# A blocked triangular inverse whose levels are put together by predicated copies instead of identity products

## The chip, the cores and the metric

The kernel runs on one core of one Trainium2 chip. The metric is the device time of one execution in microseconds (us). Engines are named as in the profile: PE is the matrix engine (PEld its weight loads), DVE the vector engine, ACT the scalar engine, POOL the GpSimd engine, SP the one that queues weight loads from memory.

## What is computed

Two transformer blocks over 512 tokens of width 1024, in fp32. The first block mixes dilated window attention with an RWKV-7 recurrence of 16 heads of 64 channels; the change lies in that recurrence and nowhere else. Cut to what matters:

```python
def step(state, inp):                                   # one token, all heads
    r_t, w_t, k_t, v_t, kk_t, a_t = inp
    sa = jnp.einsum('bhij,bhj->bhi', state, -kk_t)
    state = (state * w_t[:, :, None, :]
             + sa[..., None] * (kk_t * a_t)[:, :, None, :]
             + v_t[..., None] * k_t[:, :, None, :])
    y_t = jnp.einsum('bhij,bhj->bhi', state, r_t)
    return state, y_t
...
mu = jnp.mean(y, axis=-1, keepdims=True)
var = jnp.mean(jnp.square(y - mu), axis=-1, keepdims=True)
y = ((y - mu) * lax.rsqrt(var + LN_X_EPS)).reshape(b, s, RWKV_WIDTH)
y = y * ln_w + ln_b
y = (y + bonus) * g
```

## The kernel before

**Chunks and the inverse.** The recurrence is worked in 4 chunks of 128 tokens, for 8 pairs of heads. Inside a chunk it needs the inverse of a unit triangular 128x128 matrix per head. Both heads of a pair share one square `Z` (one head in the upper triangle, the other in the lower, -1 on the diagonal), 4 chunks side by side: a tile of 128x512. The inverse is built in levels of blocks of 2, 4, 8, ... 128 rows. A level `lv` is one turn round three engines: PE multiplies the level's blocks of the gram by the inverse so far (`level_x`: 4 products of 128x128 into bank 5, L983), ACT copies the result to SBUF (`level`, L1483), PE multiplies by the inverse again, once for the inverse and once for its transpose (`level_t`: 2 groups of 4 products into banks 4 and 6, L995), and DVE multiplies each result by a mask of sides, `smask`, which gives the operands of the next level (`level_t` on DVE, L2148, tiles `tinv` and `tinv_t`).

The old inverse has to be added to each result. Before, PE does that: ACT copies each whole result to `Tb[1]` or `TT[1]` (`whole`, L1493), and each group of `level_t` begins with a product of that copy with the identity, 512 columns wide (L992). The level's blocks of the gram are cut out by DVE, one masked copy of `Z` into `Mb` per level (`level_mask`, L2131).

**Steps.** The code runs in steps p = -2 to 7. In one step, three pairs are under way at once: a = p goes through the chunks of the recurrence (`chunk_rhs`, `chunk_solve`, `chunk_out`), b = p + 1 gets its inverse, c = p + 2 gets its keys, decays and bonus. Steps 0 to 5 have all three. Every engine takes its instructions in the order in which they are written, so the order of the calls in each engine's `step(p)` sets everything.

**Fill.** Between these pieces PE works off projections of other columns ("side halves": 8 groups of 3 products, L583 to L585, of 0.7 us a group), at places counted (`fill()`, with `SLOTS3` in steps 0 to 4, `SLOTS2` in 5). A side half is gathered in one PSUM bank, bank 0, so the next one cannot begin before ACT and DVE have read the last (`take_half` on ACT, `shift_half` on DVE, L1969 and L1970). In steps 0 to 4 the second half of a step begins in the fill after `chunk_out` of chunk 2, the third in the fill before `level_x` of level 6; both wait for DVE's `shift_half`, at its place in DVE's own order.

**Low parts.** Each weight is split into a high and a low part; in this stretch ACT makes the high part (L1258) and DVE the low part (`weights_behind`, L2031), a 128x2048 subtraction. In steps 0, 2 and 4 there is one of these per step, just before DVE's first product mask of level 3 (`level_t(b, 3, 0)`). In steps 1, 3 and 5 there are two, one before level 2 and one before `level_t(b, 5, 0)`.

**Output.** When a pair's chunks are through, the raw output is copied from PSUM (`raw_out`, L1519), its mean over each head's 64 channels is taken by a PE product (`mean`, L952), DVE subtracts it (`centred`, L2186), ACT squares, PE sums (`variance`), and so on to `normed`.

## Time and profile before

| what | value |
|---|---|
| median of 3 runs | 1886.01 us (1885.96 to 1886.76) |
| profiled execution, its own time | 1888.21 us |
| its span, first to last instruction | 1886.4 us |
| PE busy | 1809.9 us, 96% |
| DVE busy | 829.4 us, 44% |
| ACT busy | 768.5 us, 41% |
| stretch of the inverses (steps -1 to 6) | about 297 to 723 us |
| length of steps 0 to 5 (start of one inverse to the start of the next) | 52.0 to 55.4 us |

The profile gives for each engine how long it was busy, and for each instruction when it began, how long it took, and what ended the idle time before it. Products are pipelined: one of 512 columns is shown with 0.39 to 0.45 us, but the next begins 0.23 us later, so starts have to be read, not lengths. The same holds for DVE and ACT, where an instruction of 0.69 us that nothing waits for is followed by the next after 0.60 us.

### The profile page before, as it was taken

The page shows a single profiled execution, that of the slowest core. Times are in us where ns is not written, and L with a number is a line of the kernel's source. Part 1 is how long each engine was busy: PE and PEld are TensorE (multiplying, and loading weights), DVE is VectorE, ACT ScalarE, POOL GpSimd, SP SyncE. Part 2 cuts the span into 40 slices and gives each one's busy share as a digit, 9 for nine tenths or more (in the row PEclk, how much of TensorE's full clock was granted, in tenths as well). Part 3 has the DMA queues.
Part 4 walks back from the last instruction along what each step waited for, and adds up shares of the span by engine and source line. Part 5 has one row for each costly group of instructions (what it writes and reads, how often), then busy time and mean ns, then how long its engine had stood idle before and what let it go on. Part 6 is the DMA issues. An engine that isn't in the chain of part 4 may idle for free.

```text
span 1886.4 us, 22629 instructions
## 1 busy us (share of the span) xinstructions
PE 1809.9 (96%) x9636; PEld 1482.6 (79%) x9636; DVE 829.4 (44%) x1206; ACT 768.5 (41%) x1126; POOL 514.0 (27%) x115
## 2 busy tenths in 40 slices
PE   6998998999999998998999999999999999999997
PEld 5896766888888787887888888787777788888886
DVE  2015526777877765434113344515864321113243
ACT  5235555556656643234223222434663342222222
POOL 2331200000000000342434444333334334444442
PEclk8999998999999999999999999999999999999999
DMA  4631222010001002432222222221213232222221
GB/s 159 217 116 46 79 87 64 26 48 26 26 28 44 23 34 80 155 134 101 89 99 103 89 98 103 90 99 68 71 64 112 78 112 90 97 104 90 98 103 67
DMA packets 54663, 161.19 MB, mean 85 GB/s; under 512 B 3327, under 2 KB 30335, under 8 KB 39844
## 3 DMA queue, kind: packets, MB, share of 16 engines
q1 hardware_dynamic: 42476, 135.40, 20.7%
q10 hardware_dynamic: 12088, 24.35, 3.8%
q8 instruction: 76, 1.25, 0.3%
q14 instruction: 23, 0.19, 0.0%
HBM read 153.16 MB, written 10.25 MB: 87 GB/s over the span
## 4 chain that ended last, share of the span: by engine, by line
PE 82%; DVE 8%; ACT 4%; issue 4%; DMA 1%; POOL 0%; ACTq 0%; DVEq 0%
PE ps L583 22%; PE ps L585 21%; PE ps L584 21%; PE ps L995 2%; PE ps L992 1%; DVE ht_lo L1888 1%; PE ps L1072 1%; PE ps L983 1%; PE ps L905 1%; PE ps L1036 1%; PE ps L910 1%; PE ps L703 1%; DVE x_res L1905 1%; ACT y_tok L1275 1%; PE ps L713 1%
## 5 line engine op out<-in xcount | busy, mean ns | idle before, releaser
L574 POOL TENSOR_TENSOR w_lo<-w_raw,w_hi 128x2048 fp32r<-128x2048 f32 x111 | 513.8, 4629 | 1341.9 <-ACT w_hi L1258 1341.9
L583 PE MATMUL ps<-ht_hi,w_hi 128*128 128x512 f32 (+1 forms) x1304 | 526.3, 404 | 21.8 <-DVE ht_lo L1888 10.9
L585 PE MATMUL ps<-ht_hi,w_lo 128*128 128x512 f32 (+1 forms) x1304 | 501.9, 385 | 0.0
L584 PE MATMUL ps<-ht_lo,w_hi 128*128 128x512 f32 (+1 forms) x1304 | 501.3, 384 | 0.0
L1258 ACT ACTIVATE w_hi<-w_raw 128x2048 fp32r<-128x2048 f32 x126 | 241.2, 1916 | 468.0 <-PE ps L585 414.3
L583 PEld LDWEIGHTS ps<-ht_hi,w_hi 128*128 128x128 f32 x1304 | 250.4, 192 | 82.0 <-issue 26.7
L585 PEld LDWEIGHTS ps<-ht_hi,w_lo 128*128 128x128 f32 x1304 | 250.0, 192 | 48.8
L584 PEld LDWEIGHTS ps<-ht_lo,w_hi 128*128 128x128 f32 x1304 | 250.8, 192 | 39.6 <-issue 1.7
L2342 DVE TENSOR_TENSOR hid_lo<-hidden,hid_hi 128x1024 fp32r<-128x1024 f32 x27 | 129.3, 4789 | 149.1 <-ACT hid_hi L1714 149.1
L583 PE MATMUL ps<-w_hi,hid_hi 128*128 128x512 f32 x432 | 168.2, 389 | 0.0
L585 PE MATMUL ps<-w_hi,hid_lo 128*128 128x512 f32 x432 | 168.1, 389 | 0.0
L584 PE MATMUL ps<-w_lo,hid_hi 128*128 128x512 f32 x432 | 168.1, 389 | 0.0
L583 PEld LDWEIGHTS ps<-w_hi,hid_hi 128*128 128x128 f32 x432 | 81.1, 188 | 16.9
L585 PEld LDWEIGHTS ps<-w_hi,hid_lo 128*128 128x128 f32 x432 | 81.1, 188 | 16.8
L584 PEld LDWEIGHTS ps<-w_lo,hid_hi 128*128 128x128 f32 x432 | 81.1, 188 | 16.7
L583 PE MATMUL ps<-w_hi,ht_hi 128*128 128x512 f32 (+2 forms) x256 | 86.2, 337 | 2.1 <-POOL w_lo L574 2.1
L585 PE MATMUL ps<-w_hi,ht_lo 128*128 128x512 f32 (+2 forms) x256 | 85.8, 335 | 0.0
L584 PE MATMUL ps<-w_lo,ht_hi 128*128 128x512 f32 (+2 forms) x256 | 85.8, 335 | 0.0
L2351 DVE TENSOR_TENSOR hidden<-ps,gate_act 128x1024 f32<-128x1024 f32 x16 | 19.6, 1224 | 133.1 <-ACT gate_act L1753 133.1
L1753 ACT ACTIVATE gate_act<-ps 128x1024 f32<-128x1024 f32 x16 | 16.5, 1029 | 123.4 <-PE ps L585 123.4
L2148 DVE TENSOR_TENSOR tinv<-ps,sides 128x512 fp32r<-128x512 f32 x48 | 33.1, 690 | 54.1 <-PE ps L995 51.3
L2438 DVE TENSOR_TENSOR hidden<-ps,hidden 128x1024 f32<-128x1024 f32 x11 | 13.5, 1224 | 95.7 <-PE ps L585 95.7
(308 smaller groups left out, 2569.6 us busy)
## 6 DMA issues: line engine op xcount, KB each, us to landing
w_raw<-in_wpack SPq DMA_DIRECT2D x114, 1024.0 KB, 4.8
w_raw<-in_wpack SPq DMA_DIRECT2D x24, 512.0 KB, 5.3
bias_skewed_dram<-bias_rows_dram ACTq DMA_DIRECT2D x1, 3840.0 KB, 23.0
toe<-bias_skewed_dram ACTq DMA_DIRECT2D x1, 3072.0 KB, 12.9
x_res<-in_x SPq DMA_DIRECT2D x4, 512.0 KB, 5.1
merged<-gate_dram ACTq DMA_DIRECT2D x2, 1024.0 KB, 9.1
gate<-gate_dram ACTq DMA_DIRECT2D x1, 2048.0 KB, 8.8
x_res<-in_x ACTq DMA_DIRECT2D x1, 2048.0 KB, 8.7
```

What stands on the lines that cost most here:

```text
L574: nc.gpsimd.tensor_tensor(Wl[:, slot, :], raw[:, slot, :], f32(Wh[:, slot, :]), ALU.subtract).then_inc(lo_ready, 1)
L583: mm(dst, wh, ah, start=first, stop=False)
L584: mm(dst, wh, al, start=False, stop=False)
L585: return mm(dst, wl, ah, start=False, stop=last)
L703: last = nc.tensor.transpose(ps[:, 7, j * P:(j + 1) * P], LG1[i % 2][:, e, (v0 + j) * P:(v0 + j + 1) * P], ident)
L713: last = mm(ps[HD * e:HD * e + HD, 7, 3 * P:4 * P], it["vals"][e][j], PT1[e][:, j, :], start=j == 0, stop=j == nv - 1)
L905: inc(mm(bank(1), LW[c % 2][rows, 0, :], FWA[rows, 0, :], start=True, stop=True), "z_full")
L995: last = mm(ps[:, (4, 6)[k], tok(t)], (tt, x)[k], (x, tt)[k], start=False, stop=t == NT - 1)
L1258: actf(Wh[:, n % RING, :], raw[:, n % RING, :], ACT.Copy).then_inc(hi_ready, 1)
L2148: inc(v.tensor_tensor((Tb, TT)[k][0][:], src, smask(lv - 1), ALU.mult), "t_ready")
L2342: v.tensor_tensor(HIl[:, 2 * g:2 * g + 2, :], HID[:, 2 * g:2 * g + 2, :], f32(HIh[:, g % RING, :, :]), ALU.subtract).then_inc(hid_lo, 1)
L2351: v.tensor_tensor(HID[:, 2 * u:2 * u + 2, :], ps[:, 2 * (d % 2):2 * (d % 2) + 2, :], SG[:], ALU.mult).then_inc(pair_taken[d % 2], 1)
```

## The change

The result of a level is no longer added on PE. Two tiles `Wf` (fp32, in the place of `Tb[1]` and `TT[1]`) hold the inverse and its transpose; ACT fills them once per pair after level 0. After each later level DVE copies the level's blocks out of PSUM into `Wf` under a mask (`copy_predicated`), waits for that to be complete, and multiplies `Wf` by the mask of sides. So the products may leave anything outside the level's blocks, and PE can multiply by the whole gram: `Mb` is one rounded copy of `Z` (`square`, on ACT), and the masks of levels 1 to 6 go. The last level's blocks are two half-tiles per result, copied by ACT (`last_blocks`), for which `head_inverses` waits. The values are centred per head as tokens, ahead of the recurrence (`centred_values`: a sum and a subtraction on DVE), so the raw output has mean zero, and `mean` and `centred` go. Three DVE instructions of `normed` become two.

```diff
+        Wf = [place(f"inverse{k}", [P, NT, P], at=r.at - 4 * NT * P * (3 - 2 * k))[0] for k in range(2)]
...
+                if lv == 1:
+                    w("whole_ready", 4, b, 2)
                 for k in range(2):
-                    w("whole_ready", 2 * (nl - 1), b, 2 * lv - 1 + k)
-                    mm(bank((4, 6)[k]), identR[:], (Tb, TT)[k][1][:].rearrange("p t c -> p (t c)"), start=True, stop=False)
                     for t in range(NT):
                         x, tt = Xb[:, t, :], TT[0][:, t, :]
-                        last = mm(ps[:, (4, 6)[k], tok(t)], (tt, x)[k], (x, tt)[k], start=False, stop=t == NT - 1)
+                        last = mm(ps[:, (4, 6)[k], tok(t)], (tt, x)[k], (x, tt)[k], start=True, stop=True)
                     inc(last, "tt_full")
...
-                if has_a:
-                    mean(a)
                 if p == 7:
+                    w("yraw_ready", 1, a, 1)
...
+            def whole(b, k):
+
+                if k:
+                    w("m_ready", 1, b, 1)
+                    src = f32(Mb[:]).rearrange("p a b -> p (a b)")
                 else:
-                    w("t_ready", 2 * nl + 2, b, 2 * lv + 1 + k)
-                    src = bank((4, 6)[k])
-                inc(actf((Tb, TT)[k][1][:].rearrange("p a b -> p (a b)"), src, ACT.Copy), "whole_ready")
+                    w("t_ready", 2 * nl + 2, b, 1)
+                    src = bank(4)
+                inc(actf(Wf[k][:].rearrange("p a b -> p (a b)"), src, ACT.Copy), "whole_ready")
+
+            def square(b):
+
+                w("tt_full", 2 * nl - 1, b, 1)
+                w("t_ready", 2 * nl + 2, b, 2)
+                w("whole_ready", 4, b, 2)
+                inc(actf(Mb[:].rearrange("p a b -> p (a b)"), Z[:].rearrange("p a b -> p (a b)"), ACT.Copy), "square_ready")
+
+            def last_blocks(b, k):
+
+                w("tt_full", 2 * nl - 1, b, 2 * nl - 2 + k)
+                src = ps[:, (4, 6)[k], :].rearrange("p (t c) -> p t c", c=P)
+                for h in range(2):
+                    rows, cols = slice(HD * h, HD * h + HD), slice(HD - HD * h, P - HD * h)
+                    ins = actf(Wf[k][rows, :, cols], src[rows, :, cols], ACT.Copy)
+                inc(ins, "whole_ready")
...
+            def output_squares(a):
+                w("yraw_ready", 1, a, 1)
                 inc(actf(NX[:], ORW[:, a, :], ACT.Square), "ysq_ready")
...
-                    whole(b, 0, 1)
-                    whole(b, 0, 0)
+                    whole(b, 1)
+                    whole(b, 0)
+                    square(b)
...
-                    whole(b, 1, 0)
-                    whole(b, 1, 1)
                     level(b, 2)
...
-                if has_b:
-                    whole(b, 5, 0)
...
                 if has_b:
                     level(b, 6)
-                    whole(b, 5, 1)
                 if -2 < p < 7:
                     weights_behind(middle)
+                if has_b:
+                    last_blocks(b, 0)
+                    last_blocks(b, 1)
...
-            def level_mask(b, lv):
-                if lv == 1:
-                    w("tt_full", 2 * nl - 1, b, 1)
-                    w("whole_ready", 2 * (nl - 1), b, 2)
-                    w("t_ready", 2 * nl + 2, b, 2)
-                elif lv > 1:
-                    w("x_full", nl - 1, b, lv - 1)
-                inc(v.tensor_tensor(Mb[:], Z[:], lmask(lv), ALU.mult), "m_ready")
...
-                level_mask(b, 0)
+                inc(v.tensor_tensor(Mb[:], Z[:], cast4(C[:, CC["levels"]:CC["levels"] + P]), ALU.mult), "m_ready")
...
+                if lv > 1:
+                    w("whole_ready", 4, b, 2)
+                    order(v.copy_predicated(Wf[k][:], blocks(lv - 1), src))
+                    src = Wf[k][:]
                 inc(v.tensor_tensor((Tb, TT)[k][0][:], src, smask(lv - 1), ALU.mult), "t_ready")
...
                 if h:
-                    w("m_ready", nl, b, nl)
+                    w("square_ready", 1, b, 1)
+                    w("ga_ready", 2, b, 1)
                 inc(v.tensor_tensor(GA[h][:], Z[:], (upper, lower)[h], ALU.mult), "ga_ready")
...
             def head_inverses(b, k):
-                w("tt_full", 2 * nl - 1, b, 2 * nl - 2 + k)
+
+                w("whole_ready", 4, b, 3 + k)
                 for h in range(2):
-                    inc(v.tensor_tensor((Tb, TT)[k][h][:], b3((4, 6)[k]), (lower, upper)[h != k], ALU.mult), "t_ready")
+                    if h:
+                        w("t_ready", 2 * nl + 2, b, 2 * nl - 1 + 2 * k)
+                    inc(v.tensor_tensor((Tb, TT)[k][h][:], Wf[k][:], (lower, upper)[h != k], ALU.mult), "t_ready")
...
-            def centred(a):
-                w("mu_full", 1, a, 1)
-                y = ORW[:, a, :]
-                inc(v.scalar_tensor_tensor(y, bank(1 if a < PAIRS - 1 else 7), -1.0 / HD, y, ALU.mult, ALU.add), "yc_ready")
+            def centred_values(b):
+
+                w("tok_ready", 3, b, 1)
+                heads = TV[:].rearrange("p t (h c) -> p (t h) c", c=HD)
+                order(v.reduce_sum(stat[:, 32:40], heads, AX.X))
+                inc(v.scalar_tensor_tensor(heads, stat[:, 32:40].unsqueeze(2).to_broadcast([P, 2 * NT, HD]), -1.0 / HD, heads,
+                                           ALU.mult, ALU.add), "values_ready")
...
-                order(v.tensor_scalar(y, y, pcol("ln_w", a), pcol("ln_b", a), ALU.mult, ALU.add))
-                order(v.tensor_tensor(y, y, BON[a % 2][:], ALU.add))
-                v.tensor_tensor(y, y, Gb[a % 2][:], ALU.mult).then_inc(pair_open, 1)
+                order(v.scalar_tensor_tensor(y, y, pcol("ln_w", a), BON[a % 2][:], ALU.mult, ALU.add))
+                v.scalar_tensor_tensor(y, y, pcol("ln_b", a), Gb[a % 2][:], ALU.add, ALU.mult).then_inc(pair_open, 1)
                 dve.wait_ge(pair_open, a + 2)
...
-                    level_mask(b, 1)
...
-                    level_mask(b, 2)
                     level_t(b, 2, 0)
                     level_t(b, 2, 1)
...
-                    level_mask(b, 3)
                     level_t(b, 3, 0)
                 shift_half(first)
...
                     head_grams(b, 0)
-                    level_mask(b, 4)
+                    head_grams(b, 1)
                     level_t(b, 4, 0)
                     level_t(b, 4, 1)
...
-                    level_mask(b, 5)
                     level_t(b, 5, 0)
-                if has_a:
-                    centred(a)
-                if has_b:
+                    centred_values(b)
                     level_t(b, 5, 1)
-                    level_mask(b, 6)
...
-                    head_grams(b, 1)
```

In rows of the order, `tinv_120` and `tinv_121` are `Tb[0]` and `Tb[1]`, `tinv_t_122` and `tinv_t_123` are `TT[0]` and `TT[1]`, `inverse_124` and `inverse_125` are `Wf`, `level` is `Mb`, `xinv` is `Xb`, `gram_inv_116` is `Z`.

**DVE, step 2, from the masks of the products of level 0 on.** Before:

```order
L2131 TENSOR_TENSOR level<-gram_inv_116,consts 128x512 x2
L2148 TENSOR_TENSOR tinv_120<-ps,sides 128x512
L2148 TENSOR_TENSOR tinv_t_122<-ps,sides 128x512
L2172 TENSOR_TENSOR state<-ps,state 128x128
L2174 SCALAR_TENSOR_TENSOR state<-state,mid_decay,consts 128x128
L2046 SCALAR_TENSOR_TENSOR cum_decay<-consts,sig_w 128x128 x4
L2053 TENSOR_SCALAR work_t<-iclr,params_sb 128x512
L2054 SCALAR_TENSOR_TENSOR rkv<-work_t,rkv 128x512
L2031 TENSOR_TENSOR w_lo<-w_raw,w_hi 128x2048
L2131 TENSOR_TENSOR level<-gram_inv_116,consts 128x512
L2148 TENSOR_TENSOR tinv_120<-ps,sides 128x512
L1969 SCALAR_TENSOR_TENSOR rkv<-ps,one_less_mu,gate_tile 128x511
```

The same place in the changed kernel:

```order
L2148 COPY_PREDICATED inverse_124<-consts,ps 128x512
L2150 TENSOR_TENSOR tinv_120<-inverse_124,sides 128x512
L2148 COPY_PREDICATED inverse_125<-consts,ps 128x512
L2150 TENSOR_TENSOR tinv_t_122<-inverse_125,sides 128x512
L2178 TENSOR_TENSOR state<-ps,state 128x128
L2180 SCALAR_TENSOR_TENSOR state<-state,mid_decay,consts 128x128
L2053 SCALAR_TENSOR_TENSOR cum_decay<-consts,sig_w 128x128 x4
L2060 TENSOR_SCALAR work_t<-iclr,params_sb 128x512
L2061 SCALAR_TENSOR_TENSOR rkv<-work_t,rkv 128x512
L2038 TENSOR_TENSOR w_lo<-w_raw,w_hi 128x2048
L2148 COPY_PREDICATED inverse_124<-consts,ps 128x512
L2150 TENSOR_TENSOR tinv_120<-inverse_124,sides 128x512
```

The two masks of the gram ahead of level 2 and the one ahead of level 3 are gone; each product mask (L2148 before, L2150 now) has a predicated copy in front of it, and these stand ahead of `state`, the key work, the low part and `rkv<-ps` (`shift_half`).

**DVE, step 1, from the low part ahead of level 5 to the queries of the next pair.** Before:

```order
L2031 TENSOR_TENSOR w_lo<-w_raw,w_hi 128x2048
L2131 TENSOR_TENSOR level<-gram_inv_116,consts 128x512
L2148 TENSOR_TENSOR tinv_120<-ps,sides 128x512
L2186 SCALAR_TENSOR_TENSOR rwkv_out<-ps,rwkv_out 128x512
L2148 TENSOR_TENSOR tinv_t_122<-ps,sides 128x512
L2131 TENSOR_TENSOR level<-gram_inv_116,consts 128x512
L2081 TENSOR_TENSOR mid_decay<-sig_w,mid_decay 128x3
```

The same place in the changed kernel:

```order
L2038 TENSOR_TENSOR w_lo<-w_raw,w_hi 128x2048
L2148 COPY_PREDICATED inverse_124<-consts,ps 128x512
L2150 TENSOR_TENSOR tinv_120<-inverse_124,sides 128x512
L2193 TENSOR_REDUCE stat<-v_chunk 128x8
L2194 SCALAR_TENSOR_TENSOR v_chunk<-stat,v_chunk 128x512
L2148 COPY_PREDICATED inverse_125<-consts,ps 128x512
L2150 TENSOR_TENSOR tinv_t_122<-inverse_125,sides 128x512
L2088 TENSOR_TENSOR mid_decay<-sig_w,mid_decay 128x3
```

Two masks and the centring of the output went; two copies and the two instructions that centre the values came, all behind the low part.

**PE, around the products of level 4 in step 2.** Before:

```order
L584 MATMUL ps<-ht_lo,w_hi 128x512
L585 MATMUL ps<-ht_hi,w_lo 128x512
L952 MATMUL ps<-rwkv_out,consts 128x512
L992 MATMUL ps<-tinv_121,ident_r 128x512
L995 MATMUL ps<-xinv,tinv_t_122 128x128 x4
L992 MATMUL ps<-tinv_t_123,ident_r 128x512
L995 MATMUL ps<-tinv_t_122,xinv 128x128 x4
L583 MATMUL ps<-ht_hi,w_hi 128x512
```

The same place in the changed kernel:

```order
L584 MATMUL ps<-ht_hi,w_hi 128x512
L585 MATMUL ps<-ht_lo,w_hi 128x512
L586 MATMUL ps<-ht_hi,w_lo 128x512
L993 MATMUL ps<-xinv,tinv_t_122 128x128 x4
L993 MATMUL ps<-tinv_t_122,xinv 128x128 x4
L584 MATMUL ps<-ht_hi,w_hi 128x512
```

The product for the mean and the two identity products are gone; the two groups of level 4 follow the fill directly.

## Rows read from the trace of the kernel before

**Rows 1.** First part of the page: busy time, share of span, instructions.

```profile
PE 1809.9 (96%) x9636; PEld 1482.6 (79%) x9636; DVE 829.4 (44%) x1206; ACT 768.5 (41%) x1126; POOL 514.0 (27%) x115
```

**Rows 2.** One window, 280 to 735 us: length, busy PE, PEld, DVE, ACT, POOL, PEclk, DMA.

```profile
280.00:735.00 455.00, 440.38 (x2866) 359.52 (x2865) 330.84 (x606) 255.39 (x426) 0.00 (x0) 0.98 0.12 37
```

**Rows 3.** PE groups, 285 to 735 us: out<-in, count | busy, mean ns | idle.

```profile
L992 PE MATMUL ps<-tinv,ident_r 128*128 128x512 f32 x48 | 25.3, 527 | 2.4 <-ACT xinv L1483 2.4
...
L952 PE MATMUL ps<-rwkv_out,consts 128*128 128x512 f32 x14 | 7.2, 596 | 0.0
```

**Rows 4.** DVE groups, same columns; the last one from the whole span.

```profile
L2131 DVE TENSOR_TENSOR level<-gram_inv,consts 128x512 fp32r<-128x512 f32 x56 | 38.6, 689 | 16.1 <-PE ps L983 14.5
...
L2148 DVE TENSOR_TENSOR tinv<-ps,sides 128x512 fp32r<-128x512 f32 x48 | 33.1, 690 | 54.1 <-PE ps L995 51.3 <-PE ps L976 2.3
...
L2136 DVE COPY_PREDICATED gram_inv<-consts,ps 128x512 f32<-128x512 int32 x8 | 5.8, 723 | 4.4 <-issue 4.4
...
L2405 DVE TENSOR_REDUCE stat<-logits_odd 128x2 f32<-128x514 f32 x4 | 2.8, 688 | 0.1
```

**Rows 5.** DVE in order of time, steps 2 and 3: start, duration [idle <-releaser].

```profile
466.10 0.69 DVE L2148 TENSOR_TENSOR tinv<-ps,sides 128x512 fp32r<-128x512 f32 x1 [2.37 <-PE ps L995]
...
468.57 1.36 DVE L2046 TENSOR_TENSOR_SCAN cum_decay<-consts,sig_w 128x128 f32<-128x128 f32 x4
...
471.22 2.29 DVE L2031 TENSOR_TENSOR w_lo<-w_raw,w_hi 128x2048 fp32r<-128x2048 f32 x1
473.43 0.68 DVE L2131 TENSOR_TENSOR level<-gram_inv,consts 128x512 fp32r<-128x512 f32 x1
474.03 0.68 DVE L2148 TENSOR_TENSOR tinv<-ps,sides 128x512 fp32r<-128x512 f32 x1
474.63 0.74 DVE L1969 SCALAR_TENSOR_TENSOR rkv<-ps,one_less_mu,gate_tile 128x511 f32<-128x511 f32 x1
...
480.94 0.74 DVE L2059 SCALAR_TENSOR_TENSOR work_x<-rkv,params_sb 128x512 f32<-128x512 f32 x1
...
484.37 0.69 DVE L2131 TENSOR_TENSOR level<-gram_inv,consts 128x512 fp32r<-128x512 f32 x1
...
510.58 0.72 DVE L2136 COPY_PREDICATED gram_inv<-consts,ps 128x512 f32<-128x512 int32 x1 [0.62 <-issue]
...
511.34 0.72 DVE L2137 COPY_PREDICATED gram_inv<-sides,ps 128x512 f32<-128x512 int32 x1
```

**Rows 6.** PE in order of time, step 2.

```profile
465.50 0.56 PE L995 MATMUL ps<-xinv,tinv_t 128*128 128x128 f32 x4
...
472.56 0.48 PE L992 MATMUL ps<-tinv,ident_r 128*128 128x512 f32 x1
...
475.55 0.50 PE L583 MATMUL ps<-ht_hi,w_hi 128*128 128x512 f32 x1 [0.35 <-DVE rkv L1970]
```

**Rows 7.** PE in order of time, step 3.

```profile
543.02 0.56 PE L983 MATMUL ps<-tinv,level 128*128 128x128 f32 x4
```

**Rows 8.** ACT in order of time, end of step 2.

```profile
496.26 1.91 ACT L1258 ACTIVATE w_hi<-w_raw 128x2048 fp32r<-128x2048 f32 x1
```

**Rows 9.** Busy time and granted clock in three windows, columns as in Rows 2.

```profile
296.70:300.10 3.40, 1.97 (x18) 1.14 (x18) 2.64 (x5) 2.06 (x3) 0.00 (x0) 1.00 0.60 167
300.10:303.50 3.40, 3.37 (x10) 2.72 (x11) 1.98 (x3) 2.29 (x4) 0.00 (x0) 0.53 0.77 239
651.60:655.00 3.40, 2.81 (x20) 2.36 (x21) 3.40 (x7) 2.77 (x6) 0.00 (x0) 1.00 0.00 0
```

**Rows 10.** PE in order of time: two stalls.

```profile
300.13 0.95 PE L976 MATMUL ps<-ident_r,level 128*128 128x128 f32 x4 [1.46 <-DVE level L2131]
...
652.14 0.64 PE L983 MATMUL ps<-tinv,level 128*128 128x128 f32 x4 [1.10 <-DVE tinv L2148]
```

**Rows 11.** PE in order of time, step 7.

```profile
751.92 2.07 PE L952 MATMUL ps<-rwkv_out,consts 128*128 128x512 f32 x2 [3.80 <-ACT rwkv_out L1519]
```

38 lines of the change are left out of this document (12 added, 26 removed).

## The prediction

> **What bounds the kernel now.** The page first: PE is busy 96% of the span [rows 1]. The window over the inverses says the same more narrowly: of 455 us PE is busy 440, DVE 331, ACT 255 [rows 2]. So what PE no longer does would come back in full, if nothing else were close behind. The order in time shows that DVE is close behind. In step 2, DVE's mask of the products of level 1 waits 2.37 us for PE, but from there DVE works without a break through the scan at 468.57, the low part at 471.22, a mask at 473.43, the product mask of level 3 at 474.03 and the shift at 474.63 [rows 5], and PE, which has come to the next side half, waits 0.35 us for that shift [rows 6]. That chain of DVE work is already as long as what PE has to do beside it. PE's busy share cannot show this, because the wait comes at two or three places per step only.
>
> The Trainium skill says of busy matmul time that it is a bad measure of how near a kernel is to its bound, since products are pipelined (Trainium Kernel Development and Optimization, Performance Expectations). The trace bears it out in its way: PEld is busy 79%, PE 96% [rows 1].
>
> **What goes from PE.** 96 identity products (6 levels, 2 results, 8 pairs): one moves the product behind it by 0.3 us, as from L992 at 472.56 to the next group at 472.88; their shown mean of 0.53 [rows 3] overlaps that group. That is 12 x 0.29 = 3.5 us a step. The mean is two passes, 0.8 us of PE time at full clock. Together 4.3 us a step; over 8 pairs 28 us for the identities, plus some 7 for the means: 35 us of PE time at most.
>
> **What comes to DVE.** Per pair go 6 gram masks of 0.69 [rows 4], which take 0.60 from start to start (473.43 to 474.03) [rows 5], and the centring of the output; normed loses about one instruction of 0.6. There come 10 predicated copies of 128x512 out of PSUM, 0.72 each [rows 4]. Each is waited for before its mask, so that a copy takes 0.76 from start to start, as L2136 to L2137 do [rows 5]. There come also a sum over 512 columns (0.69, the nearest row has 514) [rows 4] and a subtraction, 1.34 together. Net: 10 x 0.76 + 1.34 - 6 x 0.60 - 0.60 - 0.60 = +4.1 us a step on DVE. What matters more is the place: most of the old masks ran in idle time, and the new copies stand in the turn. From PE's group to a mask that PE can use took 0.60 + 0.69 = 1.29 us (L995 at 465.50, mask at 466.10) [rows 5, 6]; now it is 0.60 + 0.76 + 0.69 = 2.05, and both results take DVE 2.72 instead of 1.28.
>
> ACT loses 10 whole copies and gains a square and four half copies: it gets lighter, at no gain, since it ends none of the waits that count here. No DMA moves, and SP's and POOL's queues stay as they are. In steps 0, 2 and 4 the last blocks stand behind a high part of 1.91 us [rows 8]; that delays head_inverses to about 1.3 us after the products, which just closes the gap in that step (below) and is counted as nothing.
>
> **Walk through step 2** (steps 0 and 4 have the same order). Level 1: PE is 0.31 earlier at L995, 465.19; DVE starts at 465.79. Two copies and masks, 2.72; state 0.60; scan, two key instructions 2.64 (468.57 to 471.22 less one gap); low part 2.21; copy and mask of level 3, 1.36; shift 0.87. Sum 10.4: the shift is ready at 476.2. PE would be there at 474.2, since two levels' identities (4 x 0.29) and no old wait stand before it: it stalls 2.0 us and starts at 476.24, where it was 475.55 before [rows 6]: +0.7. Up to the products of level 3 PE keeps that, at 479.4. From 480.04 DVE again does not rest: level 4 2.72, key work 3.43 (480.94 to 484.37) [rows 5], copy and mask 1.36, centring of the values 1.34, copy and mask 1.36, queries 1.28, copy and mask 1.36, shift 0.87: ready at 493.76. PE began that half at 493.57 before, and would now be there at 492.1: stall 1.6, +0.2. The identities of level 6 then bring it to 0 at the step's end. So with the clock at full speed a step of this kind neither gains nor loses: all 4.3 us become two stalls.
>
> **Walk through step 3** (and 1 and 5). One low part is ahead of level 2, in DVE's idle time, so the first boundary costs only 0.9 us of stall and ends even. But the second stands ahead of level 5. DVE starts level 4's copies at 533.9, where the key work ends 1.0 late, then 2.21 for the low part, and the mask for PE is ready at 543.72. PE starts `level_x` there at 543.8 instead of 543.02 [rows 7], having stalled 2.8 us. The next shift is ready at 549.8, 1.6 later than before; identities behind it give 0.4 back: +1.2 at the step's end.
>
> **The other steps.** Step 6 has no third pair, so DVE has room: every mask is early, and all comes back: -4.1. Step -1 has no recurrence, but is bound by ACT and DVE in turn: -0.3. In step 7 the mean stands right behind the raw output on a PE at half clock and takes 1.9 us (751.92, two passes of 0.85 and the switch) [rows 11]; it goes, with a small wait behind `normed`: -2.1. Sum with full clock: 3 x 0 + 3 x 1.2 - 4.1 - 0.3 - 2.1 = **-2.9 us**.
>
> **The clock.** The new stalls are of the size at which this trace shows the clock falling. After a stall of 1.46 us at 300.13 [rows 10] the granted clock is 0.53 for 3.4 us, the lower of the two levels (1.2 GHz), and that window does 3.4 x 0.47 = 1.6 us less work [rows 9]. After one of 1.10 us at 652.14 [rows 10] it stays at 1.00 [rows 9]. The stalls of 2.0 and 2.8 us lie above 1.46, that of 1.6 just above. What a fall costs is what it delays of PE's work ahead of the next thing DVE waits for; what falls in a later stall is hidden. Behind the first stall of step 2 lie 3.2 us of such work: I take 1.2 of 1.6. Behind the second, 0.8, as it does not always fall. For step 3, 0.9 (DVE has 0.5 us of its own there) and 0.5. So +2.0 for steps 0, 2, 4 and +1.4 for 1, 3, 5: 10.2 us. Total -2.9 + 10.2 = +7.3, about **+7**.
>
> The sum is made against the profiled execution, 1888.2 us with a span of 1886.4; the median of the runs is 1886.0, and I put the change on that: **1893 us**.
>
> **A rule of the skill, weighed.** The masks now read SBUF where they read PSUM. In the trace that makes no difference: L2131 reads SBUF at 689 ns, L2148 PSUM at 690 [rows 4]. The Trainium skill gives VectorE a fixed part of 58 cycles from SBUF and 120 from PSUM (VectorE: DVE Perf Modes, The TRN2 errata), 0.065 us less for each of 14 masks a step, an estimate of 0.9 us a step and 7 in eight. By it the time would be 1886. The rows are against it, and I give it 2 in 100, inside the first rival below.
>
> **Rivals.**
> - *The clock stays up.* The stalls are as walked, but PE keeps 2.4 GHz, as after 1.10 us [rows 9, 10]. Then -2.9: 1883. For it: the shorter stalls, of 1.6, are close to 1.46. Against: the stall of 1.46. 24 in 100, mostly within 0.2%.
> - *DVE's turn is shorter than walked* (faster). If the copies run at 0.60 like unwaited instructions instead of 0.76, eight of them in the unbroken stretches give 1.3 us a step, 7.7 in six steps, and the stalls of 2.0 and 1.6 go under 1.46: -2.9 - 7.7, about 1875. It decides from the point where DVE's work between the products of level 1 and the shift of step 2 is under about 9.5 us instead of 10.4. 12 in 100.
> - *PE alone is the bound.* All of 28 to 35 us comes back: 1851 to 1858. For it, the busy shares [rows 1, 2]; against it, the shift that PE waits for already [rows 6]. 6 in 100.
> - *Each stall costs a full fall.* 1.6 twice in each of six steps is 19.2 instead of 10.2: 1902. 10 in 100.
> - The forecast, 1893: 48 in 100, a small part of it within 0.2%.
>
> **Range and chances.** The difference a measurement of this kernel can tell from none is about 0.2%, 3.8 us. The range goes from the second rival to the last, 1874 to 1903, which leaves out PE alone and the ends of others. Slower by more: the last rival and most of the forecast, 0.50. Within: 0.26. Faster by more: 0.24.
>
> **What would show it.** In the profile after: no PE groups for identities or the mean; PE idle over the stretch of the inverses up from 15 us to 30 or more, its releasers DVE's `rkv` and `tinv`; in step 2 a stall of some 2 us at the second side half with DVE unbroken before it; in step 3 one of 2 to 3 us before `level_x` of level 5; clock under 1.00 behind them. Step 6 about 4 us shorter, steps 1, 3, 5 longer by 2 to 3. Wrong, if PE's stalls are under 1 us, if copies take less than 0.7 from start to start, or if the clock stays at 1.00 behind stalls of 2 us.

## The result, and the profile of the changed kernel

The changed kernel takes 1920.59 us (median of 4 runs, 1920.2 to 1921.7), the kernel before 1886.38 in the same series: a ratio of 1.018, 95% interval 1.0169 to 1.0192. That is 34.2 us slower. Forecast were 1893 us and a range of 1874 to 1903: the sign was right, the size was not, and the time lies outside the range. The profiled execution has a span of 1918.4 us, 32.0 more than that of before; the account below is made against those 32.0.

The busy line of the page, and the window that answers to [rows 2] (columns as there):

```profile
PE 1817.1 (95%) x9524; PEld 1489.1 (78%) x9524; DVE 858.9 (45%) x1238; ACT 746.4 (39%) x1086; POOL 514.0 (27%) x115
...
280.00:735.00 455.00, 417.31 (x2567) 339.16 (x2568) 340.32 (x601) 221.45 (x365) 0.00 (x0) 0.90 0.11 33
```

112 matmuls are gone from the whole (9636 to 9524), and yet PE is busy 7 us longer. The clock column says why: 0.90 over the inverses, where it was 0.98. Steps -1 to 5 are cut by the first product of the grams of each inverse; of before, then of after:

```profile
296.65:671.12 374.47, 365.73 (x2417) 298.08 (x2417) 289.69 (x540) 221.22 (x372) 0.00 (x0) 0.99 0.11 32
```

```profile
294.89:707.60 412.71, 378.37 (x2321) 307.21 (x2321) 317.00 (x570) 202.70 (x337) 0.00 (x0) 0.89 0.10 29
```

These seven steps grow by 38.2 us. Ahead of the first cut 1.8 us are gained, behind the last 4.5 (steps 6 and 7): 38.2 - 1.8 - 4.5 = 32. The 1.8 is spread (the first cut lies at 293.2 to 296.7 us in the traces of this case). So the loss is in the seven steps. PE's idle time there goes from 8.7 us (374.47 less 365.73) to 34.3. Who is waited for (columns: engine and line, releaser, us in total, times, longest), from 280 to 820 us:

```profile
PE ps L981 <- DVE tinv L2150: 15.4, 10, 4.6
PE ps L584 <- DVE rkv L1977: 11.9, 8, 1.9
...
PE ps L993 <- DVE tinv_t L2150: 2.6, 2, 1.6
```

All are DVE's turns: the mask (L2150) behind a copy, and the shift that frees the next side half (L1977). On PE, in order of time, the two stalls of step 2, the long one of step 3 and that of step 5 (idle time in brackets):

```profile
485.40 0.80 PE L584 MATMUL ps<-ht_hi,w_hi 128*128 128x512 f32 x1 [1.88 <-DVE rkv L1977]
...
506.23 0.76 PE L584 MATMUL ps<-ht_hi,w_hi 128*128 128x512 f32 x1 [1.43 <-DVE rkv L1977]
...
559.65 0.65 PE L981 MATMUL ps<-tinv,level 128*128 128x128 f32 x4 [2.51 <-DVE tinv L2150]
...
682.48 1.09 PE L981 MATMUL ps<-tinv,level 128*128 128x128 f32 x4 [4.56 <-DVE tinv L2150]
```

DVE at the first of them, with no idle time between these rows: low part, copy, mask, shift.

```profile
480.91 2.29 DVE L2038 TENSOR_TENSOR w_lo<-w_raw,w_hi 128x2048 fp32r<-128x2048 f32 x1
483.12 0.72 DVE L2148 COPY_PREDICATED inverse<-consts,ps 128x512 f32<-128x512 int32 x1
483.87 0.69 DVE L2150 TENSOR_TENSOR tinv<-inverse,sides 128x512 fp32r<-128x512 f32 x1
484.48 0.74 DVE L1976 SCALAR_TENSOR_TENSOR rkv<-ps,one_less_mu,gate_tile 128x511 f32<-128x511 f32 x1
```

A copy takes 0.75 us from start to start, as walked. The new part is what the clock does around the stalls (a stall is idle time of PE ahead of a product that has to wait). Four windows, placed on the stretches in which the clock stands at its lower level (1.2 GHz; such a stretch is called a fall, and its time low clock), two of step 2, one of step 3, one of step 5:

```profile
485.10:491.90 6.80, 6.50 (x25) 5.92 (x25) 3.76 (x10) 1.10 (x4) 0.00 (x0) 0.50 0.00 0
505.50:512.30 6.80, 6.07 (x23) 4.90 (x23) 4.06 (x11) 3.02 (x3) 0.00 (x0) 0.50 0.28 81
560.10:573.80 13.70, 13.70 (x57) 11.70 (x57) 9.00 (x19) 5.07 (x8) 0.00 (x0) 0.50 0.01 1
679.60:696.60 17.00, 14.12 (x57) 12.14 (x58) 11.51 (x21) 4.38 (x7) 0.00 (x0) 0.50 0.00 1
sum 88.50, PE 80.89 PEld 69.41 DVE 59.05 ACT 27.82 POOL 0.00; mean PE 8.09 PEld 6.94 DVE 5.90 ACT 2.78 POOL 0.00
```

The sum is over all ten such stretches of the seven steps: 88.5 us, and PE is busy in 80.9 of them. The falls of the changed kernel are 3.4, 6.8, 13.7 and 17.0 us long; one of the ten is the short one, in step 0. In the kernel before there are two in the seven steps, both in step -1, the second with its stall:

```profile
300.30:303.70 3.40, 3.40 (x12) 2.75 (x12) 1.98 (x3) 2.26 (x4) 0.00 (x0) 0.51 0.73 230
...
317.47 0.80 PE L992 MATMUL ps<-tinv,ident_r 128*128 128x512 f32 x1 [2.40 <-ACT xinv L1483]
...
317.40:324.20 6.80, 6.73 (x24) 5.96 (x24) 4.66 (x8) 1.72 (x4) 0.00 (x0) 0.50 0.00 0
```

If busy time at half clock is counted as half work, the clock costs 40.4 us (half of 80.9) against 5.1 (half of 10.1), 35.4 more. The account of the seven steps is then: idle +25.6, clock +35.4, and PE's work at full clock -22.7. The last is what is left of the growth of busy time (378.4 - 365.7 = +12.6) after the 35.4, so that the three add up to the 38.2 by the way they are made. A value for the work from other runs is near it: 84 identity products at 0.20 us (x12_no_identity) and six means at 0.6 to 0.8 (x3_values) are 20 to 22 us, an estimate.

### The profile page after: what moved, and what is told of

Same layout as the page of the kernel before. It is cut to its first block, busy times and chain, and to the rows that moved or that the text cites. A ratio compares the mean times of both kernels' runs of the same rounds, so it can differ in the third digit from the quotient of the medians.

```text
span 1918.4 us, 22478 instructions
## 1 busy us (share of the span) xinstructions
PE 1817.1 (95%) x9524; PEld 1489.1 (78%) x9524; DVE 858.9 (45%) x1238; ACT 746.4 (39%) x1086; POOL 514.0 (27%) x115
## 4 chain that ended last, share of the span: by engine, by line
PE 77%; DVE 11%; issue 6%; ACT 4%; DMA 1%; POOL 0%; ACTq 0%; DVEq 0%
PE ps L584 22%; PE ps L585 21%; PE ps L586 21%; DVE inverse L2148 2%; PE ps L993 1%; DVE ht_lo L1895 1%; PE ps L1071 1%; PE ps L981 1%; PE ps L906 1%; PE ps L1035 1%; PE ps L704 1%; DVE x_res L1912 1%; ACT y_tok L1273 1%; PE ps L1025 1%; PE ps L725 1%
## 5 line engine op out<-in xcount | busy, mean ns | idle before, releaser
L584 PEld LDWEIGHTS ps<-ht_hi,w_hi 128*128 128x128 f32 x1304 | 251.6, 193 | 92.2 <-issue 34.2
L2148 DVE COPY_PREDICATED inverse<-consts,ps 128x512 f32<-128x512 int32 x80 | 58.2, 728 | 57.7 <-PE ps L993 57.5
L1481 ACT ACTIVATE xinv<-ps 128x512 fp32r<-128x512 f32 x48 | 28.6, 597 | 73.4 <-PE ps L981 73.4
```

The costliest lines, as they stand in the source:

```text
L584: mm(dst, wh, ah, start=first, stop=False)
L1481: inc(actf(Xb[:].rearrange("p a b -> p (a b)"), bank(5), ACT.Copy), "x1_ready")
L2148: order(v.copy_predicated(Wf[k][:], blocks(lv - 1), src))
```

## The experiments

All times are medians; ratios are against the kernel before on the same chip. The stretch is steps -1 to 5, cut as above.

| kernel | us | ratio, interval | stretch, us | PE busy | clock |
|---|---|---|---|---|---|
| before | 1886.4 | | 374.5 | 365.7 | 0.99 |
| changed | 1920.6 | 1.0180 [1.0169, 1.0192] | 412.7 | 378.4 | 0.89 |
| x1_warm | 1892.2 | 1.0034 [1.0021, 1.0046] | 385.8 | 370.6 | 0.97 |
| x2_identity | 1904.9 | 1.0103 [1.0084, 1.0123] | 396.4 | 368.2 | 0.97 |
| x7_delay | 1894.4 | 1.0044 [1.0027, 1.0060] | 383.7 | 370.6 | 0.97 |
| x9_stalls | 1915.8 | 1.0157 [1.0139, 1.0175] | 404.4 | 373.7 | 0.95 |
| x11_behind | 1921.6 | 1.0185 [1.0171, 1.0199] | 414.2 | 380.2 | 0.94 |
| x12_no_identity | 1868.3 | 0.9896 [0.9881, 0.9911] | 363.3 | 349.6 | 0.98 |
| x4_low | 1900.3 | 1.0080 [1.0064, 1.0096] | 393.0 | 359.2 | 0.95 |
| x5_turn | 1897.9 | 1.0066 [1.0050, 1.0083] | 387.8 | 356.8 | 0.96 |
| x3_values | 1881.1 | 0.9974 [0.9965, 0.9984] | 375.3 | 364.1 | 0.98 |
| x13_levels | 1904.1 | 1.0099 [1.0085, 1.0113] | 392.6 | 361.6 | 0.96 |
| x14_last | 1884.9 | 0.9994 [0.9985, 1.0003] | 374.3 | 362.3 | 0.98 |

### Is it the clock? x1_warm

```
+   WARM = {p: (8, 0, 6) if p % 2 == 0 else (4, 10, 0) for p in range(5)}; WARM[5] = (0, 18, 0)
+   def warm(p, place):
+       for _ in range(WARM.get(p, (0, 0, 0))[place]):
+           mm(bank(5), identR[:], HTh[:, 0, :], start=True, stop=True)
    # place 0 ahead of the second half, 1 ahead of level_x(b, 5), 2 ahead of the third half
```

> The changed kernel, with spare 128x512 products written into PE's bank 5 (they are overwritten, and the output stays the same) at the places where PE stalls in it: in steps 0, 2, 4 eight ahead of the second side half and six ahead of the third, in steps 1 and 3 four ahead of the second half and ten ahead of level_x of level 5, in step 5 eighteen there. At 0.23 us each they take 1.84, 1.38, 0.92, 2.3 and 4.1 us, a little less than the stalls of 1.88, 1.43, 0.95, 2.5 and 4.56. Theory A (PE's new stalls themselves are worth about what the walk gave them, near 0 over all steps; the rest of the loss is the clock, which falls behind them and stays at half for 3 to 17 us each time): the clock over 280 to 765 us goes from 0.90 back to 0.98 or more, and the time to 1880 to 1888 us. Rival B (DVE's longer turn is the bound by itself, the clock only accompanies it): 1915 to 1922 us, with the clock up.

PE does the spare products while it would have waited, and the half behind them starts without a wait. PE in order of time, step 2, and the stretch:

```profile
476.03 2.11 PE L1082 MATMUL ps<-ht_hi,ident_r 128*128 128x512 f32 x8
477.99 0.50 PE L584 MATMUL ps<-ht_hi,w_hi 128*128 128x512 f32 x1
...
295.88:681.64 385.76, 370.64 (x2408) 298.67 (x2408) 316.47 (x570) 202.16 (x337) 0.00 (x0) 0.97 0.10 31
```

1892.2 us: 28 of the 34 us come back, though nothing that PE waits for became faster and PE does some 20 us of useless work (88 products at 0.23). Rival B falls. Theory A is the nearer one, but the time is 4 us above its range (the seven runs spread from 1888.2 to 1897.1). In steps 1 and 3 a stall of 1.35 us came up ahead of the third half, which I had not filled. In step 3 the clock falls for 6.8 us at it, from 551.4 on, 1.2 us before the stall ends; in step 1 it does not fall. Step 5 has another fall of 6.8 us, behind a stall of only 0.78. Steps 0, 2 and 4, with the clock at 1.00, are each 0.5 us longer than before, step 1 is 2.1 longer. So the stalls alone are not worth nothing: of the 11.3 us by which the stretch is longer than before, the clock is some 4 (18.4 us of busy time at half clock against 10.1, halved), and some 7 are left at full clock.

### Is it the length of the stalls? x2_identity, x7_delay, x9_stalls, x11_behind

x2_identity puts a spare product at each old place, where the level's own products overwrite it:

```
  for k in range(2):
+     mm(bank((4, 6)[k]), identR[:], Xb[:].rearrange("p t c -> p (t c)"), start=True, stop=True)
      for t in range(NT):
```

> The changed kernel, with a spare identity product of 128x512 at each place where one was removed (12 a step; it is overwritten by the level's products, and the output stays the same). PE gets its 0.29 us each back, 3.5 us a step. Theory A: the stalls of 1.88 and 1.43 us become about 1.3 and 0.7, that of 2.5 about 1.6, and some of the falls of the clock go: 1895 to 1912 us. Rival B (DVE bounds each turn, the clock is no matter): 1918 to 1924 us. Rival C (what kept the clock up before was these dense products and not the absence of stalls): clock back at 0.98 though stalls above 1.3 us stay, 1885 to 1892 us.

1904.9 us, inside theory A's range, but for another reason than A's. Up to step 4 the stalls at the three places are 1.40 and 0.97 us in the even steps and 1.99 in the odd ones, and behind that of 1.99, longer than the one of [rows 10] behind which the clock fell, the clock stays up (step 3, PE and the window from there on):

```profile
552.22 0.64 PE L981 MATMUL ps<-tinv,level 128*128 128x128 f32 x4 [1.99 <-DVE tinv L2151]
...
552.20:562.00 9.80, 8.85 (x62) 7.41 (x63) 9.32 (x20) 4.84 (x8) 0.00 (x0) 1.00 0.00 0
```

Over steps 0 to 4 the clock is low for 3.4 us, for 64.9 in the changed kernel. Step 5 is the exception: a stall of 4.09 us and a fall of 17 us, as in the changed kernel (4.56 and 17). So the identity products did not shorten that one.

x7_delay makes a stall in the kernel before:

```
      level_t(b, 3, 0)
+     if p in (0, 2, 4):
+         for _ in range(2):
+             order(v.reduce_max(stat[:, 60:61], CS[:], AX.X))
  shift_half(first)
```

> The kernel before, with two sums over 512 columns (their result is not used) put on DVE ahead of the shift that frees the second side half, in steps 0, 2 and 4 only: 1.45 us of DVE. PE's stall of 0.35 us there becomes 1.8 us. Theory A: the clock falls behind each of the three stalls as in the changed kernel and stays at half for 3 to 7 us: each stall costs its 1.45 us and 2 to 3.3 us more, together 1896 to 1901 us. Rival B or C (the identity products are still there, so the clock stays up): 3 x 1.45 us, 1890 to 1891 us.

```profile
479.13 0.50 PE L583 MATMUL ps<-ht_hi,w_hi 128*128 128x512 f32 x1 [1.80 <-DVE rkv L1970]
...
480.80:484.20 3.40, 3.40 (x15) 3.01 (x14) 1.06 (x2) 1.18 (x5) 0.00 (x0) 0.51 0.00 0
```

1894.4 us, between the two expectations. Steps 2 and 4 grow by 3.03 us each: 1.45 of stall and 1.6 of a fall that lasts 3.4 us (step 0 has one of 6.8 and grows by 4.7). The changed kernel has at this place a stall of 1.88, nearly the same, and falls of 3.4, 6.8 and 6.8 us in steps 0, 2 and 4. So there is a fall at a stall of this size with the identity products too. It is shorter in steps 2 and 4 and longer in step 0, 13.7 us in all against 17.1: from this run alone one can't say that the identity products shorten a fall.

x9_stalls is x2_identity with one such sum ahead of both shifts in the even steps and ahead of level 5 in the odd ones, so that its stalls up to step 4 are longer than most of those of the changed kernel (in step 5 the longest is 1.23 us, for 4.56).

> The kernel of x2_identity (the changed kernel with a spare identity product at each old place) with 0.72 us more on DVE (a sum whose result is not used) ahead of the shift of the second and of the third half in steps 0, 2, 4 and ahead of level 5 in steps 1, 3, 5, so that the stalls are 2.1, 1.7 and 2.7 us, no shorter than in the changed kernel, while PE has its dense products back. By the sizes alone 3 x 1.44 + 3 x 0.72 = 6.5 us more than x2_identity, 1911 us. If the length of the stalls decides whether and for how long the clock falls: it falls as in the changed kernel, 60 us or more at half, 1930 to 1945 us. If the removed dense products count (rival C): the clock stays near 0.98, 1909 to 1918 us.

Step 3, the longest stall and the window behind it, which in the changed kernel holds 13.7 us at half clock:

```profile
562.18 0.63 PE L981 MATMUL ps<-tinv,level 128*128 128x128 f32 x4 [2.71 <-DVE tinv L2151]
...
562.18:580.00 17.82, 16.89 (x113) 13.84 (x114) 15.28 (x32) 8.58 (x16) 0.00 (x0) 1.00 0.01 1
```

2.71 us of stall and no fall (step 1 has the same stall and one of 3.4 us); in step 2, stalls of 2.12 and 1.69 with 3.4 us of low clock behind each, where the changed kernel has 6.8 behind 1.88 and 1.43. Over steps 0 to 4 the low clock is 20.5 us, for 64.9 in the changed kernel. 1915.8 us lies in rival C's range, though the clock of the stretch, 0.95, is below the 0.98 that it gave. The length of the stall alone doesn't decide.

x11_behind leaves the stalls and puts spare products behind them (six behind the first piece of the second and of the third half, twelve behind the products of level 5).

> The changed kernel with spare 128x512 products behind PE's stalls, not ahead of them: in steps 0, 2, 4 six behind the first piece of the second half and six behind that of the third, in steps 1, 3, 5 twelve behind the products of level 5. They add 1.4 us each at full clock (2.8 the twelve) and leave the stalls about as long as they are. If the low clock lasts as long as PE's work behind the fall is thin: the low stretches of 6.8 us become 3.4 and those of 13.7 become 3.4 to 6.8, and the time is 1905 to 1920 us in spite of 17 us more work. If its length has nothing to do with that work: the low stretches stay, 1932 to 1940 us.

Its large stalls are those of the changed kernel to 0.01 us. In step 2 there is no fall at the stall of 1.88, in step 3 that of 13.7 us is one of 6.8 (each time PE, then a window behind it):

```profile
485.55 0.50 PE L584 MATMUL ps<-ht_hi,w_hi 128*128 128x512 f32 x1 [1.88 <-DVE rkv L1988]
...
485.50:492.40 6.90, 6.85 (x43) 5.89 (x43) 5.09 (x11) 1.67 (x4) 0.00 (x0) 1.00 0.00 0
```

```profile
558.18 0.64 PE L981 MATMUL ps<-tinv,level 128*128 128x128 f32 x4 [2.52 <-DVE tinv L2161]
...
558.18:565.40 7.22, 7.22 (x31) 6.64 (x32) 5.96 (x11) 3.84 (x6) 0.00 (x0) 0.56 0.01 2
```

That step 2 has no fall is not the work of the spare products behind it alone: in the changed kernel that fall begins at 485.0, 0.4 us before the stall ends. The lengths say more. Of the ten places of the seven steps eight have a shorter fall or none and two the same, 51.2 us in all for 88.8. So some 19 us less are lost, and 17 us of useless work are added: the time, 1921.6, is that of the changed kernel, 1.6 us above the range that I had given. Together x2_identity, x9_stalls and x11_behind show that the work of PE around a stall decides with it whether the clock falls and for how long. What exactly the clock answers to, they do not tell. Equal stalls have unequal falls: 1.88 us in the changed kernel has 3.4 us in step 0 and 6.8 in steps 2 and 4, and 1.35 us in x1_warm has a fall in one step and none in another. Each of these edits also moves the stalls in time, and whether the moment at which a stall comes plays a part was not tested by itself.

### What is the change worth at full clock? x12_no_identity, x4_low, x5_turn, x6_turn_act

x12_no_identity takes the identity products out of the kernel before and adds nothing, so that its inverse lacks the blocks of the earlier levels.

```
-   mm(bank((4, 6)[k]), identR[:], (Tb, TT)[k][1][:].rearrange("p t c -> p (t c)"), start=True, stop=False)
```

> The kernel before, leaving out the identity products of the levels (the inverse then lacks the blocks set before, so this part of the result is not computed rightly; all other work and every wait is as before). PE loses 3.5 us a step, DVE and ACT nothing. It tells how much of those 28 us DVE's turn leaves, without the copies. If PE were the bound alone: 1858 us. By the walk without copies: the shift of the second half, which PE waits 0.35 us for already, takes about 1.2 us of each even step, level 5 of each odd step about as much: 1862 to 1872 us if the clock stays at 0.98. If the removal of dense products alone lets the clock fall at stalls of 1.0 to 1.5 us: low clock of 40 us or more, 1880 to 1895 us.

Step 1 of before, then of x12_no_identity, neither with a fall:

```profile
399.63:454.25 54.62, 54.53 (x367) 44.62 (x366) 43.58 (x81) 32.12 (x56) 0.00 (x0) 1.00 0.08 23
```

```profile
395.85:448.43 52.58, 52.14 (x355) 42.34 (x354) 43.46 (x81) 32.10 (x56) 0.00 (x0) 1.00 0.08 24
```

2.4 us of PE's busy time go with twelve products: 0.20 each, not 0.29. The time is 18.2 us shorter. So that much was to be had from PE, if it cost DVE nothing. This run also shows what the missing products do to the clock when nothing is put on DVE. The kernel before has no fall in steps 0 to 4; here there are two, of 6.8 us in step 0 and 3.4 in step 2, each at a stall of 0.36 us (the next one before it, 0.80 us, lies 17 us back), while step 4 has the same stalls and no fall. Step 0, PE and the window:

```profile
377.42 0.76 PE L583 MATMUL ps<-ht_hi,w_hi 128*128 128x512 f32 x1 [0.36 <-DVE rkv L1969]
...
377.30:384.10 6.80, 6.68 (x25) 5.51 (x26) 3.35 (x9) 3.98 (x5) 0.00 (x0) 0.50 0.38 102
```

x4_low moves two of DVE's low parts in the changed kernel (in steps 0, 2, 4 from ahead of level 3 to ahead of level 4, in 1, 3, 5 from ahead of level 5 to ahead of head_inverses), nothing else.

> The changed kernel, with two of DVE's low parts moved: in steps 0, 2, 4 from ahead of the mask of level 3 to ahead of level 4's, behind both head grams, where DVE idles 3.2 us; in steps 1, 3, 5 from ahead of level 5 to ahead of head_inverses, where it idles 2.5 us. Nothing else changes. Theory A: the stalls of 1.88 us at the second half and of 2.5 and 4.56 us before level_x of level 5 go, and with them the longest stretches of the low clock; stalls of 1.4 to 2 us at the third half stay: 1870 to 1890 us. Rival B (DVE's work as a whole bounds the step): no change, 1915 to 1922 us.

x5_turn does more: shifts ahead of masks, a head gram and the centring of the values ahead of head_inverses in even steps.

> The changed kernel with DVE's order made for the new waits, nothing else: low parts in steps 0, 2, 4 ahead of level 4, in steps 1, 3, 5 in two halves around the gram of level 6; each shift of a side half ahead of the masks that came before it (and of the queries); in the even steps the second head gram and the centring of the values ahead of head_inverses. By the walk DVE is then on time at both shifts. Theory A: no stall above 1 us before the third half in steps 0 to 4, the clock at 0.97 or more, and the 4.3 us a step that PE lost become free: 1850 to 1868 us. Rival B (DVE's work as a whole is the bound, a stall only moves, to gate_z at the end of the odd steps above all): 1880 to 1900 us.

x4_low takes 1900.3 us: the stall of 2.5 us in step 3 is 0.32 now, but new ones of 1.7 (step 2, level 5) and 1.35 (step 3, third half) came. Neither range holds it. x5_turn takes 1897.9. Its step 2 has the clock at 1.00 all through, PE busy 52.6 us for 54.6 before, and yet it is 1.8 us longer than before (56.94 for 55.11); the waits went to the masks:

```profile
478.58 0.64 PE L981 MATMUL ps<-tinv,level 128*128 128x128 f32 x4 [0.63 <-DVE tinv L2150]
...
491.16 0.64 PE L981 MATMUL ps<-tinv,level 128*128 128x128 f32 x4 [1.68 <-DVE tinv L2150]
...
497.83 0.63 PE L981 MATMUL ps<-tinv,level 128*128 128x128 f32 x4 [1.07 <-DVE tinv L2150]
...
456.81:513.75 56.94, 52.58 (x354) 41.81 (x353) 44.99 (x85) 30.95 (x52) 0.00 (x0) 1.00 0.13 41
```

Neither of the two orders of this DVE work that I tried lets PE have its gain: a stall moved to the next mask. The time lies in the range of rival B of x5_turn, but it is not DVE's work as a whole that bounds the step: DVE is busy in 45.0 of the 56.9 us. The stalls are at the turns, where PE waits for the copy and the mask of its own last products. That these turns bound a step at full clock is what the runs bear out.

x6_turn_act is x5_turn with ACT's last blocks ahead of its high part of 1.91 us:

```
+   last_blocks(b, 0); last_blocks(b, 1)
    if -2 < p < 7:
        weights_behind(middle)
-   if has_b:
-       last_blocks(b, 0); last_blocks(b, 1)
```

> The kernel of x5_turn, with ACT's last blocks ahead of its high part of 1.91 us in place of behind it (steps 0, 2, 4, 6). If the prediction was right to count that order as nothing: within 3 us of x5_turn. If head_inverses, which waits for the last blocks, sets the end of the even steps: 4 to 8 us less.

The spans of the two profiled executions are 1895.1 and 1895.0 us, their steps agree to 0.05; the medians (1897.9 and 1894.2) differ by 3.7 us, a little more than the 3 that I had given and less than the 4 to 8 of the other case, and the four runs of x6_turn_act alone spread over 4.7. The traces show nothing that the order on ACT is worth, as the prediction counted it; the medians don't exclude a small gain.

### Which part of the change? x3_values, x13_levels, x14_last

x3_values is the kernel before with the values centred as tokens and no mean:

```
-   inc(mm(bank(norm_bank(a)), ones_head, ORW[:, a, :], start=True, stop=True), "mu_full")
...
      level_t(b, 5, 0)
-   centred(a)
+   centred_values(b)
      level_t(b, 5, 1)
```

> One part of the change alone: the kernel before, with the values centred as tokens, without the mean of the output on PE, and with the shorter normed. The levels of the inverse keep their identity products and masks. On PE 0.8 us a step goes over 7 steps and 1.9 us in step 7, on DVE the sum and subtraction of 1.34 us stand where the centring of 0.6 stood. Theory A (the loss of the changed kernel is in the levels): the stretch becomes a little shorter or stays, 1878 to 1886 us, stalls as before, no new fall of the clock. Rival: the 0.7 us more on DVE ahead of the third half makes a stall there: 1888 to 1892 us.

x13_levels is the other part alone: the changed kernel with the mean on PE, the centring of the output on DVE and the longer normed.

> The other part of the change alone: the levels with predicated copies and without identity products and masks, while the mean stays on PE and the centring of the output on DVE as before, at their old places. If the two parts add up: the change is +34.2 us and the values alone gave -5.4, so +39.6, 1926 us. If the loss is in their meeting (1.34 us of centring between the copies of level 5): 1905 to 1915 us.

The values alone give 5.4 us: 1881.1, faster by 0.26% (0.16 to 0.35). The levels alone cost 17.6. The two do not add up: 12 us by the sum, 34 together. Both expectations of x13_levels missed, the second by 1 us only. PE in x13_levels, step 1:

```profile
429.56 1.10 PE L953 MATMUL ps<-rwkv_out,consts 128*128 128x512 f32 x2 [0.36 <-DVE kk L2079]
...
433.98 0.64 PE L985 MATMUL ps<-tinv,level 128*128 128x128 f32 x4 [1.04 <-DVE tinv L2154]
```

Here the mean (0.8 us, L953) stands where the changed kernel waits 2.52 us in one piece: 0.36, the mean, then 1.04. At this place the clock stays up; it falls 6 us later, at a stall of 1.03 us ahead of the third half, for 3.4 us, where the changed kernel has 13.7 (in step 3 x13_levels has no fall at all). With the levels changed, the mean stands in time that PE has to spare; without it two small stalls are one long one. PE's idle time over the stretch is nearly the same, 31.0 us against 34.3, but the clock is low for 30.7 us against 88.8: the 22 us between the sum and the two together are for the most part in the clock. That the split stall is the reason in every step is not shown.

x14_last takes x3_values and drops the identity products of the last level alone, whose blocks ACT copies.

```
+   mm(ps[:, (4, 6)[k], tok(t)], (tt, x)[k], (x, tt)[k], start=lv == nl - 1, stop=lv == nl - 1 or t == NT - 1)
...
+   actf((Tb, TT)[k][1][rows, :, cols], src[rows, :, cols], ACT.Copy)   # h = 0, 1
```

> The kernel of x3_values, and at the last level alone no identity products: PE's block products go into empty banks, and ACT copies only the two off-diagonal blocks of each result into the whole inverse, from which DVE's four last masks are taken. DVE gets no copy. PE loses 0.58 us a step, ACT gains 1.5. If PE is free to take it: 4 to 5 us less than x3_values, 1876 to 1878 us. If head_inverses, which now waits for ACT's blocks, comes late for refine_u or delays normed and gate_z: 1881 to 1890 us.

1884.9, no gain over x3_values: the time is in the range of the second expectation. Steps 0 to 4 are shorter by 0.1 to 0.2 us each, not by 0.58, and step 5 has 10.2 us of low clock behind its stall of 2.06. Why the median is 3.8 us above that of x3_values is not shown.

### A faster version: x10_values_low, x8_before_low, x16_values_warm, x17_all_warm

The trace of x3_values has a fall of 13.7 us, in step 5, behind this stall. (The profiled execution, 1884.67 us, is the slowest of ten with a median of 1881.1, so that a usual one may have less of it.)

```profile
643.68 0.64 PE L979 MATMUL ps<-tinv,level 128*128 128x128 f32 x4 [2.05 <-DVE tinv L2144]
```

x10_values_low moves DVE's low part away from there (and a shift ahead of a mask), x8_before_low does that to the kernel before.

```
- weights_behind(first)
+ if p not in (1, 3, 5):
+     weights_behind(first)
...
      grams(b, 1)
+     if p in (1, 3, 5):
+         weights_behind(first)
      head_inverses(b, 0)
```

> The kernel of x3_values (values centred as tokens, the levels as before) with DVE's order mended at the places where its trace still stalls: the low part ahead of level 5 in steps 1, 3, 5 moved ahead of head_inverses, and the shift that frees the second half ahead of the mask of level 3. In the trace of x3_values step 5 has a stall of 2.05 us before level_x of level 5 and 13.7 us of low clock behind it (step 5 takes 57.9 us, against 52.0 before), steps 0, 2, 4 and 1, 3 a stall of 0.35 each. Expected if those are what is left: step 5 at 51 to 52 us, 1870 to 1877 us. If DVE's tail in the odd steps takes it back (gate_z waits for normed): 1879 to 1885 us.

> The kernel before with the same two moves of DVE's order as x10_values_low and nothing else, to see what the order is worth by itself. Its trace has stalls of 0.35 us in steps 0, 2, 4 and one of 1.1 us in step 5: 1883 to 1886.5 us, if nothing new waits; up to 1890 us if the tail of the odd steps does.

1883.0 (ratio 0.9979, 0.9970 to 0.9988) and 1887.0 (1.0000, 0.9991 to 1.0009). Both lie in the range of their second case (1879 to 1885, and up to 1890). The order by itself is worth nothing. Step 5 of x10_values_low is 53.4 us long instead of the 57.9 of that slow execution, gate_z now waits 0.73 us for normed there, and falls of 3.4 and 6.8 us stay around it. Why the median is no better than that of x3_values is not shown beyond this.

x16_values_warm is x3_values with spare products in the idle times that it keeps; x17_all_warm adds x10's moves and x14's last level.

```
+   if p == -1 and t == 2: spare(9, 2)      # ahead of level_t(b, 2)
...
+   if p == 5: spare(8, 5)                  # ahead of level_x(b, 5)
...
+   if p == 6: spare(5, 1)                  # ahead of chunk_out(a, 0)
...
+   spare(8, 5)                             # step 7, ahead of the half
...
+   spare(14, 5)                            # step 7, ahead of the branch
```

> The kernel of x3_values with spare 128x512 products (0.23 us each, overwritten or never read) in the idle time that its trace shows before the clock falls: nine ahead of the products of level 2 in step -1 (stall 2.4 us), eight ahead of level_x of level 5 in step 5 (2.05 us), five ahead of the first chunk_out of step 6 (1.64 us), eight at the start of step 7 (2.46 us), fourteen ahead of the branch work in step 7 (3.8 us). The trace of x3_values has 30.6 us of low clock over 280 to 780 us. If low clock costs half its length and the spare products keep it away: 10 to 15 us less than x3_values, 1866 to 1872 us. If they delay what they stand before as much as they help: 1879 to 1883 us.

> x16_values_warm together with the moves of x10_values_low and the last level of x14_last (no spare products in step 5). By the same account 1864 to 1872 us; no better than x16_values_warm if the moves and the last level are worth nothing, as x10 and x14 say.

The window 285 to 780 us of before, then of x16_values_warm:

```profile
285.00:780.00 495.00, 477.04 (x3050) 388.88 (x3049) 344.84 (x621) 267.83 (x444) 4.60 (x1) 0.98 0.15 48
```

```profile
285.00:780.00 495.00, 482.99 (x3128) 396.52 (x3127) 349.70 (x624) 271.32 (x445) 10.05 (x3) 1.00 0.16 50
```

The clock is at 1.00, and the time 1876.3 us, ratio 0.9948 (0.9934 to 0.9962): 10 us faster than before and 5 faster than x3_values, half of the least that I had expected. A part of the rest is in step -1: the nine products did not take the place of the stall of 2.40 us ahead of level 2, which is 3.34 behind them, and the step is 2.1 us longer than in x3_values. Why ACT's copy came later there was not followed up. x17_all_warm is the same within its spread: 1875.7, 0.9945 (0.9933 to 0.9958).

## The prediction, step by step

- **PE's gain, 4.3 us a step.** Too large. An identity product is worth 0.20 us (x12_no_identity), not 0.29, and the mean 0.6 to 0.8 (x3_values: busy 53.9 for 54.5 in step 1). PE's work fell by some 23 us over seven steps, 3.2 a step, where the sum had 29.
- **DVE's copies at 0.76.** Right: 0.75 from start to start. Right too that the source makes no difference; DVE groups of the changed kernel, columns as in [rows 3], the copy and the masks out of SBUF and PSUM:

```profile
L2148 DVE COPY_PREDICATED inverse<-consts,ps 128x512 f32<-128x512 int32 x80 | 58.2, 728 | 57.7 <-PE ps L993 57.5
L2150 DVE TENSOR_TENSOR tinv<-inverse,sides 128x512 fp32r<-128x512 f32 x40 | 27.7, 692 | 1.4
...
L2150 DVE TENSOR_TENSOR tinv<-ps,sides 128x512 fp32r<-128x512 f32 x8 | 5.5, 691 | 1.9 <-PE ps L973 1.6
```

The Trainium skill's smaller fixed cost for an SBUF source (VectorE: DVE Perf Modes, The TRN2 errata) does not show: 692 ns from SBUF, 691 from PSUM.
- **The stalls.** Right for steps 0 to 4: 2.0 and 1.6 forecast for step 2, 1.88 and 1.43 measured (and 0.48 before level 5); 0.9 and 2.8 for step 3, 0.95 and 2.51 measured. The second half of step 2 starts 22.1 us into it, 0.8 later than before; forecast 0.7. The third starts 3.6 later (43.0 us into the step, for 39.3), forecast 0.2: between the two lies the first fall. So the 1.43 is the stall of a PE that had worked at half clock in between, and its nearness to 1.6 is in part luck.
- **Step 5.** The sum took it as like step 3. It has one side half less, so PE has less to do beside the same DVE work: its stall is 4.56 us, and it grows by 8.1 instead of 2.6.
- **The full-clock sum.** For steps -1 to 5 it was -0.3 + 3 x 1.2 = +3.3; idle +25.6 less work 22.7 is +2.9. The match is luck in part: PE's work fell by 7 us less than the sum had, and its idle time grew by 7 less (25.6, where the sum has 29 + 3.3), measured with falls in between. x1_warm, with the clock up, is the better measure: the steps with the clock at 1.00 throughout are longer by 0.5 (0, 2, 4) and 2.1 us (1), forecast 0 and 1.2, and the stretch by some 7, forecast 3.3.
- **Steps 6 and 7.** Forecast -6.2, measured -4.5. Up to the wait of 2.46 us at the start of step 7, 4.8 us are gained, forecast 4.1. The 2.1 of the mean in step 7 did not come: from that wait to the end the changed kernel is 0.3 us longer.
- **The clock, +10.2. This is the step that failed**: it measured +35. Two things in it were wrong. I took every fall to last as long as that of [rows 9], 3.4 us; nine of the ten lasted 6.8, 13.7 or 17.0. The old trace already had a longer one, 6.8 us from 317.4 on, at a stall of 2.40 us, which I had not read. And I took about half of the cost (10.2 of 12 x 1.6) to be hidden or not to come, where PE was busy in 80.9 of 88.5 us. The rival of a full fall each time (1902) had the same 3.4. What I had not thought of is that the change also takes away what surrounds the stalls: the identity products and the mean. Put back (x2_identity, x9_stalls), steps 0 to 4 have 3.4 and 20.5 us of low clock for 64.9, and taken out alone (x12_no_identity) they bring falls at stalls of 0.36 us. Step 5 is not explained by that (x2_identity keeps its 17 us).
- **ACT's last blocks, nothing.** Right by the traces (x6_turn_act).
- **The rivals.** PE alone and a shorter DVE turn were rightly small; the clock did not stay up; the full fall was the nearest, and still 19 us short.

## What to carry to other kernels

A product that only copies is not free to remove if the engine that takes its place is near its turn: here PE gave 0.20 us for each and DVE paid 0.75 in the same turn. And on a PE that is near its bound, count a new stall with the clock that falls behind it, and look at what the change removes around the stall: a fall read from one place of the old trace as 3.4 us was 7 to 17 us long at nine of ten places when the stalls were new and the dense work beside them was gone. Where a wait can't be removed, a few spare products in it are cheap to try: they won back 28 of 34 us here and 5 more in the best version.

## What the runs showed of the hardware

- The clock stayed at 1.00 behind a stall of 2.71 us (x9_stalls, step 3) and fell at one of 1.43 in the changed kernel and at one of 0.36 in x12_no_identity. The stretches at half clock were 3.4 to 17.0 us long.
- Twelve products of 128x512 with a fixed weight cost 2.4 us of busy PE (x12_no_identity), though the rows of the kernel before show them with 0.45 to 0.53 each.
- In the changed kernel a predicated copy of 128x512 out of PSUM takes 0.73 us on DVE, the mask behind it 0.69, out of either memory. The sums of 8 groups of 64 columns take 0.68.

Open is what the clock answers to exactly, whether the moment of a stall counts, and how much of x1_warm's last 6 us is the stall that I did not fill.
